# Conv feed-forward entry: squares summed on GpSimd, the gate tile in halves, r copied by ScalarE, two new buffers

## What is computed

```python
def rmsnorm(x, g):
    y = xf * lax.rsqrt(jnp.mean(xf * xf, axis=-1, keepdims=True) + EPS)
    return (y * g).astype(x.dtype)

def conv_ffn(h, past_f, w_up, conv_w, w_down):
    z = h @ w_up
    g, up = jnp.split(z, 2, axis=-1)
    gc, new_past_f = causal_dwconv(g, past_f, conv_w)     # 3 taps
    return (jax.nn.silu(gc) * up) @ w_down, new_past_f

for l in range(DEPTH):                                     # DEPTH = 2
    x = x + mixer(rmsnorm(x, norm_mix[l]))                 # l = 0: conv module + gMLP, l = 1: gated conv
    x = x + conv_ffn(rmsnorm(x, norm_ffn[l]), ...)         # D = 1024, D_FF = 2816
y = rmsnorm(x, norm_final)
```

## Time and profile before

| | us |
|---|---|
| median of 3 runs | 2216.91 (2215.58 to 2218.7) |
| the profiled execution | 2216.46 |
| its span, first to last instruction | 2214.7 |
| PE busy | 2140.4 |
| DVE busy | 1473.9 |
| POOL busy | 882.0 |
| ACT busy | 651.1 |

### The profile page before, as it was taken

One profiled execution on the slowest core, in us unless ns is written; L12 is line 12 of the kernel. 1 busy time (PEld: TensorE's weight loads), 2 busy tenths in 40 slices (PEclk: granted clock), 3 DMA queues, 4 the chain that ended last, 5 costly groups with the idle time before them and its releaser, 6 DMA issues. The chain is left out here.

```text
span 2214.7 us, 35320 instructions
## 1 busy us (share of the span) xinstructions
PE 2140.4 (97%) x15116; PEld 2127.6 (96%) x15116; DVE 1473.9 (67%) x1849; ACT 651.1 (29%) x906; POOL 882.0 (40%) x540
## 2 busy tenths in 40 slices
PE   7997999899999999999999999998999999999996
PEld 6987999899999999999999999998999999999996
DVE  5999967876666766666743534478666666666666
ACT  4443234322323222223401110243222332222233
POOL 4764323543444344344422211234444443444344
PEclk9998999999999999999999999999999999999998
DMA  4110211111111111111111111111111111111112
GB/s 157 39 39 30 99 69 39 39 39 58 58 52 46 39 58 49 48 58 58 39 48 48 38 48 48 39 38 39 58 39 58 58 48 47 41 58 39 58 41 79
DMA packets 33996, 115.31 MB, mean 52 GB/s; under 512 B 3824, under 2 KB 7408, under 8 KB 33840
## 3 DMA queue, kind: packets, MB, share of 16 engines
q1 hardware_dynamic: 33840, 113.06, 15.1%
HBM read 108.42 MB, written 4.62 MB: 51 GB/s over the span
## 5 line engine op out<-in xcount | busy, mean ns | idle before, releaser
L597 PE MATMUL psum<-xs_hi,w_hi 128*128 128x264 f32 (+1 forms) x3728 | 1117.1, 300 | 47.1 <-DVE xs_lo L1563 16.2
L599 PE MATMUL psum<-xs_hi,w_lo 128*128 128x264 f32 (+1 forms) x3728 | 1113.5, 299 | 0.0
L598 PE MATMUL psum<-xs_lo,w_hi 128*128 128x264 f32 (+1 forms) x3728 | 1110.0, 298 | 0.0
L1023 POOL TENSOR_TENSOR w_lo<-raw,w_hi 128x512 fp32r<-128x512 f32 (+1 forms) x358 | 592.6, 1665 | 992.5 <-ACT w_hi L1201 641.1
L597 PEld LDWEIGHTS psum<-xs_hi,w_hi 128*128 128x128 f32 x3728 | 706.8, 190 | 53.7 <-issue 11.4
L598 PEld LDWEIGHTS psum<-xs_lo,w_hi 128*128 128x128 f32 x3728 | 707.3, 190 | 0.0
L599 PEld LDWEIGHTS psum<-xs_hi,w_lo 128*128 128x128 f32 x3728 | 706.2, 189 | 0.0
L597 PE MATMUL psum<-act_hi,w_hi 128*128 128x352 f32 x1152 | 372.7, 324 | 0.1
L599 PE MATMUL psum<-act_hi,w_lo 128*128 128x352 f32 x1152 | 372.7, 323 | 0.0
L598 PE MATMUL psum<-act_lo,w_hi 128*128 128x352 f32 x1152 | 369.9, 321 | 0.0
L1574 DVE TENSOR_TENSOR x<-psum,x 128x704 f32<-128x704 f32 x208 | 185.1, 890 | 188.4 <-PE psum L599 185.8
(11 more groups left out here) (229 smaller groups left out, 1775.5 us busy)
## 6 DMA issues: line engine op xcount, KB each, us to landing
raw<-slabs SPq DMA_DIRECT2D x188, 512.0 KB, 3.2
x<-x_t SPq DMA_DIRECT2D x16, 528.0 KB, 6.7
y_t<-x SPq DMA_DIRECT2D x6, 528.0 KB, 3.3
y_t<-x SPq DMA_DIRECT2D x3, 352.0 KB, 2.3
x<-mix SPq DMA_DIRECT2D x1, 512.0 KB, 3.2
x<-bs SPq DMA_DIRECT2D x1, 256.0 KB, 3.7
tail_hi<-consts SPq DMA_DIRECT2D x1, 132.0 KB, 10.8
const<-consts SPq DMA_DIRECT2D x1, 130.0 KB, 4.4
```

Source lines behind the costliest of these rows:

```text
L597: nc.tensor.matmul(out, w_hi[:, w], hi, start=start, stop=False, skip_group_check=reopen)
L598: nc.tensor.matmul(out, w_hi[:, w], lo, start=False, stop=False, skip_group_check=reopen)
L599: return nc.tensor.matmul(out, w_lo[:, w], hi, start=False, stop=stop, skip_group_check=reopen)
L1023: nc.gpsimd.tensor_tensor(w_lo[:, slab], src, w_hi[:, slab].bitcast(F32), ALU.subtract).then_inc(weights_ready, 1)
```

## The change

Phases 1 and 3 alone are changed in their work.

- POOL sums squares 1 to 6 at both `last_down` places (`EARLY`), in pairs behind each of the three weight slabs; DVE is left with one addition. The squares go to two buffers in turn, so ACT's square m waits for POOL's sum m - 2.
- The gate tile is written in halves: PE starts its first half before x's last tile is added, and `rms_stats` stands right behind the gate tile.
- ACT copies the gate tile before `t_high` of the second combination, and copies r out of PSUM itself, ahead of the last `t_high`.
- DVE scales the up tile, makes the last weight sum and t1's low parts before it scales the gate tile and convolves it; in the second pair it takes the results in another order.
- The P1 copy of the second pair and the first silu write to buffers of their own (`first_p1`, `first_factor`) in place of work's.

```diff
+FIRST_UP_READ = 2
...
+    if (b, q) == (0, 1):
+        which = {C22_READ: 1, C21_READ: 2, C11_READ: 3, C12_READ: 4}[which]
     return _unit_at(p, EVAC0, 4, 8, ("pair", b, q)) + which
...
-POOL_SUMS = 3
-DVE_SUMS = KD - POOL_SUMS - 1
+
+
+EARLY = [3, 6, 3, 6, 3, 3, 3]
+LATE = [KD - 1 - n for n in EARLY]
+EARLY0 = [sum(EARLY[:k]) for k in range(8)]
+LATE0 = [sum(LATE[:k]) for k in range(8)]
...
-        t_sq = [sumsq[:], conv_in[0][:, 0:COLS], conv_out[0][:, 0:COLS], prod[0], prod[1]]
-        t_sq += t_sq[1:4]
+        first_p1 = quarter(slots_lo, 2)
+        first_factor = slots_lo[:, 0:COLS]
+        t_sq = [sumsq[:]] + [conv_in[0][:, 0:COLS], prod[0]] * 4
...
-                pe.wait_ge(tile_evacuated, EVAC0[p])
+                pe.wait_ge(tile_evacuated, EVAC0[p] - 1)
                 a11, a12 = weights(0), weights(1)
                 x_bank = X_BANKS[0]
-                for kp in range(KP):
-                    pe.wait_ge(xg_ready, KD * p + 2 * kp + 1)
-                    block_product(a11, X_B11, x_bank, kp, kp == 0, False)
-                    block_product(a11, X_B12, Y_BANK, kp, kp == 0, False)
-                    pe.wait_ge(xg_ready, KD * p + 2 * kp + 2)
-                    block_product(a12, X_B21, x_bank, kp, False, kp == KP - 1)
-                    block_product(a12, X_B22, Y_BANK, kp, False, kp == KP - 1).then_inc(tile_done, 1)
+
...
+                def gate_tile(kps, first_bank, x_even, x_odd):
+                    for kp in kps:
+                        pe.wait_ge(xg_ready, KD * p + 2 * kp + 1)
+                        block_product(a11, x_even, first_bank, kp, kp == 0, False)
+                        pe.wait_ge(xg_ready, KD * p + 2 * kp + 2)
+                        last = block_product(a12, x_odd, first_bank, kp, False, kp == KP - 1)
+                    last.then_inc(tile_done, 1)
+
+                gate_tile(range(KP - 1), x_bank, X_B11, X_B21)
+                pe.wait_ge(tile_evacuated, EVAC0[p])
+                gate_tile(range(KP - 1), Y_BANK, X_B12, X_B22)
+                gate_tile([KP - 1], x_bank, X_B11, X_B21)
+                gate_tile([KP - 1], Y_BANK, X_B12, X_B22)
+                pe.wait_ge(squares_summed, LATE0[p + 1])
+                rms_stats(p, psum[:, 7, 0:ROW_TILES])
                 a21 = weights(2)
                 for kp in range(KP):
                     last = block_product(a21, X_B11, Z_BANK, kp, kp == 0, False)
                 last.then_inc(tile_done, 1)
-                pe.wait_ge(squares_summed, DVE_SUMS * (p + 1))
-                rms_stats(p, psum[:, 7, 0:ROW_TILES])
...
+                if second:
+                    pe.wait_ge(part_copied, 3 * (n - 1) + 3)
+                elif q == 1:
...
+                if second:
+                    pe.wait_ge(tile_evacuated, pair_read(p, 0, 0, FIRST_UP_READ))
+                elif q == 1:
...
-                lo(p - 1, n0 + 1)
-                early_squares(p, p, 1, t_sq)
-                lo(p - 1, n0 + 2)
-                early_squares(p, p, 2, t_sq)
-                early_squares(p, p, 3, t_sq)
-                lo(p - 1, n0 + 3)
+                for kp in range(3):
+                    lo(p - 1, n0 + 1 + kp)
+                    early_squares(p, p, 2 * kp + 1, t_sq)
+                    early_squares(p, p, 2 * kp + 2, t_sq)
...
-                    if m > 4:
-                        act.wait_ge(early_sum, POOL_SUMS * p + m - 4)
+                    if m > 2:
+                        act.wait_ge(early_sum, EARLY0[p] + m - 2)
...
-                elif kp == 1:
-                    act.wait_ge(squares_summed, DVE_SUMS * p + 2)
-                else:
+                elif kp > 1:
                     act.wait_ge(t_made, 4 * (KP * s + kp - 2) + 1)
...
-                t_high(p, 1)
-                make_b11(p, 3)
                 act.wait_ge(tile_done, group_done(p, 0, 0, GATE_DONE))
-                act.wait_ge(squares_summed, DVE_SUMS * (p + 1))
+                act.wait_ge(squares_summed, LATE0[p + 1])
...
                 entry_hi(p, 0, 1, 0)
+                t_high(p, 1)
+                make_b11(p, 3)
                 t_high(p, 2)
                 entry_hi(p, 0, 1, 1)
+                act.wait_ge(r_spread, p + 1)
+                nc.scalar.activation(r_rows[:, 0:1024], psum[:, 6:8, :].rearrange("p a b -> p (a b)"),
+                                     ACT.Copy).then_inc(r_ready, 1)
+                nc.scalar.activation(r_rows[:, 1024:COLS], psum[:, Y_BANK, 300:300 + ROW_REST],
+                                     ACT.Copy).then_inc(r_ready, 1)
                 t_high(p, 3)
...
+                f = factor if (b, q) != (0, 0) else first_factor
                 act.wait_ge(conv_tap, t * 3 + 3)
-                nc.scalar.activation(factor[:, 0:SEQ], conv_out[0][:, 0:SEQ], ACT.Silu)
-                nc.scalar.activation(factor[:, SAMPLE:COLS], conv_out[0][:, SAMPLE + GAP:GAP_COLS],
+                if (b, q) == (0, 0):
+                    act.wait_ge(t2_ready, KP * (l + 1))
+                nc.scalar.activation(f[:, 0:SEQ], conv_out[0][:, 0:SEQ], ACT.Silu)
+                nc.scalar.activation(f[:, SAMPLE:COLS], conv_out[0][:, SAMPLE + GAP:GAP_COLS],
...
-                nc.scalar.activation(two(half(prod[q], 1)), halves_of(x_bank), ACT.Copy).then_inc(part_copied, 1)
+                    act.wait_ge(t4_ready, KP * (s + 1))
+                p1 = first_p1 if before == FIRST else half(prod[q], 1)
+                nc.scalar.activation(two(p1), halves_of(x_bank), ACT.Copy).then_inc(part_copied, 1)
...
-                act.wait_ge(tile_evacuated, pair_read(p, b, q, C11_READ))
+                if before != FIRST:
+                    act.wait_ge(tile_evacuated, pair_read(p, b, q, C11_READ))
                 nc.scalar.activation(two(half(prod[q], 1)), halves_of(Z_BANK), ACT.Copy).then_inc(part_copied, 1)
...
                 g = conv_in[0]
                 late_squares(p, p, KD - 1, t_sq)
-                dve.wait_ge(squares_summed, DVE_SUMS * (p + 1))
+                dve.wait_ge(squares_summed, LATE0[p + 1])
                 clear_history(g)
                 combine(p, 0)
                 combine(p, 1)
+                mean_square(p, psum[:, 7, 0:ROW_TILES])
                 sums(p, 0, 1, 1)
                 combine(p, 2)
-                mean_square(p, psum[:, 7, 0:ROW_TILES])
                 sums(p, 0, 1, 2)
                 combine(p, 3)
-                copy_r(p, psum[:, Y_BANK, 300:300 + ROW_REST])
+                dve.wait_ge(r_ready, 2 * (p + 1))
+                dve.wait_ge(tile_done, group_done(p, 0, 0, FIRST_DONE))
+                for i, bank in enumerate((Z_BANK, X_BANKS[0])):
+                    dve.tensor_tensor(two(half(prod[0], i)), halves_of(bank), two(half(r_rows[:], i)),
+                                      ALU.mult).then_inc(tile_evacuated, 1)
+                sums(p, 0, 1, 3)
+                t1_low(p)
                 dve.wait_ge(part_copied, 3 * n + 3)
                 dve.tensor_tensor(g[:, 2:2 + SEQ], g[:, 2:2 + SEQ], r_rows[:, 0:SEQ], ALU.mult).then_inc(tile_evacuated, 1)
                 sample = g[:, 2 + SAMPLE + GAP:2 + GAP_COLS]
                 dve.tensor_tensor(sample, sample, r_rows[:, SAMPLE:COLS], ALU.mult).then_inc(tile_evacuated, 1)
-                dve.wait_ge(tile_evacuated, pair_read(p, 0, 0, C22_READ))
+                dve.wait_ge(tile_evacuated, pair_read(p, 0, 0, C12_READ))
                 dve.wait_ge(t4_ready, KP * (p // 2) + 2)
                 at_f = p // 2 * FF_TILES
                 conv_start(CONV0[p], 0, at_f * 3, "conv_f_w", at_f * 2, "state_f", new_f, at_f * 4)
                 conv_tap_k(p, 0, 0, 1)
                 conv_tap_k(p, 0, 0, 2)
-                sums(p, 0, 1, 3)
-                dve.wait_ge(tile_done, group_done(p, 0, 0, FIRST_DONE))
-                for i, bank in enumerate((Z_BANK, X_BANKS[0])):
-                    dve.tensor_tensor(two(half(prod[0], i)), halves_of(bank), two(half(r_rows[:], i)),
-                                      ALU.mult).then_inc(tile_evacuated, 1)
-                dve.wait_ge(tile_evacuated, pair_read(p, 0, 0, C12_READ))
-                t1_low(p)
...
+                f = factor if (b, q) != (0, 0) else first_factor
+                dve.tensor_tensor(prod[q], prod[q], f, ALU.mult).then_inc(product_done, 1)
...
-                if leads:
...
+                if before == FIRST:
+                    c22()
                     sums(p, after[1], after[2], 1, step_of(p, unit, 4))
-                if follows:
-                    product(p, before[1], before[2])
-                if q == 0 and b >= 2:
-                    hidden_lo(p, b - 1, 1)
-                dve.wait_ge(tile_done, group_done(p, b, q, 1))
-                dve.wait_ge(product_done, ACT0[p] - ACT0[1] + 2 * b + q)
-                dve.wait_ge(part_copied, 3 * n + 1)
-                dve.tensor_tensor(two(g0), halves_of(Y_BANK), two(half(prod[q], 1)),
-                                  ALU.add).then_inc(tile_evacuated, 1)
-
```

(63 more changed lines are left out.)

20 lines of the change are left out of this document (5 added, 15 removed).

## The result

| | before | after |
|---|---|---|
| median of 5 runs, us | 2217.39 (2215.58 to 2218.7) | 2226.99 (2224.4 to 2230.5) |
| ratio of the runs | | 1.0043, 95% interval 1.0031 to 1.0056 |
| span of the profiled execution | 2214.7 | 2222.6 |
| DVE, POOL busy | 1473.9, 882.0 | 1465.0, 902.0 |

The change makes the kernel 9.6 us slower; 2230 was forecast, in a range of 2221 to 2243. The profiled execution, 2224.40, is the fastest of the five, 2.6 us under their median.

A forecast was written before the change was run, and what follows sets the result against it. PE is busy 97% of the span, so only its waits and slow stretches can be given back. 6.4 - 2.8 + 2.0 + 1.0 = 6.6 us an entry, 13.2 in the kernel, gives 2230 from the median 2216.91; range 2221 to 2243.

The forecast's parts named there:

- Squares on POOL: Ahead of the gate tile, two slabs late by 2.6 us each and a gate tile wait longer by 1.2: +6.4 an entry.
- DVE's earlier total of the squares: With three additions less on DVE the total is ready earlier, but this hides behind the gate tile's 11.7 us.
- The clock behind these waits: In `last_down`, PE was taken to run at full clock behind the new waits of 2.4 to 2.9 us.
- a rival of 0.16 for half: Each new `last_down` wait puts PE to half clock, 2.0 us each, three times an entry: +12, 2242; chance 0.16.
- half clock behind the new waits: Sign that the forecast is wrong: PE at half clock behind the new waits; no size given for the sign.
- Group 4 at E + 35.2: In the second pair, group 4 starts 35.2 us after the gate tile's end, before 38.0: 2.8 us given back an entry.
- each meeting of DVE and POOL: In the entry, DVE waits about 1.1 us per POOL instruction met, 7 to 9 times: 7.5 to 9.9 us.
- a wait for the P1 copy: In the second pair, PE waits for ACT's P1 copy, 3 to 4 us, as it also does for the second copy.
- Half clock behind group 4: After PE's waits in the second pair, a slow stretch now lies behind group 4: +2.0 us an entry (0 to 2.0).
- Small waits later: Group 1 or 2 of the pair behind the second may wait, its first result being read late: +1 us (0 to 2).
- The buffers: `first_p1` and `first_factor` remove ACT's wait for DVE's first reading, which is not the last one: no cost, no gain.
- DVE's list as the bound of the entry: DVE's list replaces the old waits up to group 4, so 2.8 us of the 10.2 lost there comes back.

The follow-up runs named there:

- its own twin with the slabs first: The kernel before with six squares' sums on GpSimd, each slab's low half ahead of the sum that would hold it up, entry as before: 2212.75 us.
- squares alone: The kernel before with only the change's six squares' sums on GpSimd in the last down projections, VectorE keeping the final sum: 2228.33 us.
- slab 2 early: The changed kernel with the second pair's third slab rounded by ACT before the last `t_high`, its low part made by POOL before the last `t4_lo`: 2234.08 us.
- silu later: The changed kernel with that third slab early on ACT and POOL, and the first gate's silu behind the second pair's second copy on ACT: 2227.22 us.
- slabs first: The changed kernel with GpSimd making each slab's low half before the squares' sum that would hold it up: 2209.42 us.
- the run with the pause: The changed kernel with slabs' low halves before the squares' sums, and VectorE waiting for the third slab's low half before t1's low halves: 2215.07 us.
- silu last: The changed kernel with slabs' low halves before the squares' sums, and silu behind the second and third copies on ScalarE: 2209.59 us.
- entry alone: The changed kernel with the squares as before (three sums on GpSimd, old buffers and order), so only the entry's changes: 2213.92 us.

## Why the prediction was right, and where it was wrong

*Squares on POOL, +6.4 an entry (5.8 to 7.3):* the waits grew by 6.0 and 5.8, and the gate tile starts 6.6 and 6.5 us later. Right, by its own steps: the addition waits for ACT's square, the slab behind it is late. The new waits of 2.3 to 2.4 us lie just under the 2.4 to 2.9 that were forecast, since the slab took 2.35 us and the addition 2.06. The runs put the whole part at 11.4 us for both entries, 15.6 to 16.8 against its own twin with the slabs first. One step of it was wrong: that DVE's earlier total of the squares gives nothing, because it hides behind the gate tile. ACT's gate copy waits for that total, and by the twin it is worth about 2.5 us an entry with the old entry left as it was.

*The clock behind these waits, taken as full, with a rival of 0.16 for half:* it was neither. Over the four profiles that have them (changed, squares alone, slab 2 early, silu later) 24 waits of 2.3 to 2.7 us stand at these places, and behind 10 of them the next 4 us ran at 0.57 to 0.65, behind the other 14 at 1.00. The 4 us behind the first wait in squares alone, to be held against the line from 340.70 above:

```profile
341.30:345.30 4.00, 4.00 (x15) 4.00 (x16) 1.02 (x1) 2.15 (x3) 2.44 (x1) 0.57 0.40 131
```

A slow one costs 1.6 us (two jobs in 15.7 us instead of 14.1), so by an estimate 4 us a kernel, 2.0 an entry, was left out of the sum. The Trainium skill, "TensorE: Matmul & The Clock Gate" (section "HAM oscillation — how this bites in real kernels"), describes a kernel in which PE is clocked down again by each of its waits of several microseconds for data. The traces agree for the long ones: all 24 waits of 3.0 to 6.6 us in the two entries, over all profiles, have 0.50 to 0.65 behind them. They show it for part of the shorter ones too, and in the kernel before for the two of 1.68 us behind the norm's one-column products (above). Those products were followed by a low clock at some places even with no wait behind them: 0.61 and 0.60 in the profile of the slabs first, 1.00 at both in that of the changed kernel. The forecast had named half clock behind the new waits as a sign that it was wrong; it came in part.

*Group 4 at E + 35.2 (33.6 to 36.0), E being the end of the gate tile, here 380.97:* it started at 33.5, which gives back 4.5 us and not 2.8, and the convolution ended at 30.6, where 31.3 to 33.7 was forecast. (Seven waits of 1.1 us are 7.7, not 7.5; nothing hangs on it.) The forecast priced each meeting of DVE and POOL as a wait of DVE's. Here is **the step that failed**: where POOL's instruction comes second, it waits for the whole run of DVE's instructions. That takes the delay out of DVE's list and puts it ahead of group 2, as the 3.2 us wait for the slab. The forecast had a wait for the P1 copy there; that copy was ready. The Trainium skill, "SBUF — State Buffer" (section "SBUF: two separate sides"), has whichever starts first keep the ports for its whole instruction, and the other blocked. The traces agree on who waits. In the changed kernel DVE's L1889 started at 400.37 and POOL's instruction at 400.38, which took 5.44 us. In the run with slab 2 early POOL was first (two low parts from 406.56), and the same L1889 took 1.14 us in place of 0.68:

```profile
406.56 3.00 POOL L1042 TENSOR_TENSOR w_lo<-raw,w_hi 128x512 fp32r<-128x512 f32 x2 [1.01 <-ACT w_hi L1218]
```
```profile
407.27 1.14 DVE L1889 TENSOR_TENSOR raw<-raw 128x512 f32<-128x512 f32 x1
```

But the block is not of one instruction: it is of six, and the run with the pause brought it to 1.83 us.

*Half clock behind group 4, +2.0:* it stood behind group 2 and cost little, because PE was early for group 4. In phase 1 the second copy was done at 413.80 and group 4 started at 414.51 without a wait, so 0.7 us was paid; in phase 3 PE still waited 0.29 us there, so none was. *Small waits later, +1:* behind group 4 3.0 us (1.17 + 0.88 + 0.97) against 1.8 (0.67 + 1.12), +1.2.

*The buffers* were not tried by themselves; that P1 and silu's buffers cost or give nothing stays an argument.

*DVE's list as the bound of the entry:* true in a narrower sense than was said. It holds group 2, through POOL's blocked instruction, and group 4, through silu's place in ACT's list. It does not hold the work itself: with one wait and silu two copies later the same instructions take 7.2 us less.

So the sign and the main term were right. The forecast for an entry was 6.6; by the runs it was 4.8 (9.6 / 2). Up to group 4 the entry gave back 1.7 us more than forecast, the half clock behind it cost 1.3 to 2.0 less, and about 2.0 of half clock behind the late slabs was not counted. These errors go against each other, so that the time came within 3.0 us of 2230 is in part luck.

## What to carry to other kernels

When work is moved to an engine that also feeds the matmuls, write what feeds them first and put the moved work behind it: here the same six additions cost 11 us in one order and gave 5.4 in the other. Where VectorE and GpSimd hold each other up, look for unbroken runs of the one, and put its pause where the other has something that TensorE waits for; and before an early wait is taken away, see what the next one absorbs: here the half clock behind a wait was nearly free while another wait followed it, and cost 1.8 to 2.6 us where none did.

## What the runs showed of the hardware that was not expected

A GpSimd instruction of 128 x 512 took 5.44 us, and not 1.3 to 1.8, beside six VectorE instructions without a gap; it ended 1.16 us behind the last of them. It took 5.43 to 5.46 us there in both phases of all four profiles that have this order (changed, slabs first, silu last, entry alone). The same wait, 2.36 or 2.37 us, at the same place left TensorE's clock at 1.00 in one profile and at 0.57 in another. The norm's one-column products, with no wait behind them, were followed by a low clock at some places and not at others. Why was not found for either.
